# One decoder layer on one core: another order of splits, taps, scaled keys and key sums inside the loop over four heads

## The chip, the core and the metric

The kernel runs on one core of a Trainium2 chip. The metric is the device time of one execution in microseconds (us), lower is better. The core has five engines that run their own queues in order and meet through semaphores: TensorE (matrix products), VectorE and ScalarE (elementwise work), GpSimd (here mostly a queue that issues DMAs) and SyncE (the queue that loads weights).

## What is computed

One layer of a hybrid decoder on 512 prompt tokens and 8 x 4 sample tokens, model width 1024: a convolution branch and an mLSTM memory with 4 heads (value width 512, key width 256), merged by gates, then an MLP. The part that the change touches is the memory of one head:

```python
def step(carry, xs):                       # a chunk of tokens
    ...
    w_intra = jnp.exp(D - m_t[:, :, None, :])
    w_inter = jnp.exp(inter - m_t)
    s = jnp.einsum('bthk,bshk->btsh', qc, kc) * w_intra
    num = jnp.einsum('btsh,bshv->bthv', s, vc) + w_inter[..., None] * jnp.einsum('bhvk,bthk->bthv', C, qc)
    den = jnp.sum(s, axis=2) + w_inter * jnp.einsum('bhk,bthk->bth', n, qc)
    h = num / jnp.maximum(jnp.abs(den), jnp.exp(-m_t))[..., None]
    ...
    C_new = dec[..., None, None] * C + jnp.einsum('bsh,bshv,bshk->bhvk', wk, vc, kc)
    n_new = dec[..., None] * n + jnp.einsum('bsh,bshk->bhk', wk, kc)
    return (C_new, n_new, m_new), h
...
c = lax.conv_general_dilated(full, w_dw[:, None, :], ...) + b_dw     # 31 taps per channel
...
hm = hm.reshape(B, T, D_M).astype(x.dtype) * jax.nn.sigmoid(o)
```

## The kernel before

All weights come as chunks of 1024 x 128 values (512 KB) in the order of their use. SyncE loads a chunk into one of two places of `wraw`, as soon as the chunk two places ahead has been split. A **split** makes two tiles of it: ScalarE writes `whi` (line 512, a rounded copy), then VectorE writes `wlo` (line 830, what the rounding lost). Both lie in rings of four, so the split of chunk k also waits until the product of chunk k-4 is done. `split(k)` in the head loop is this pair of steps, one on each engine's queue; it runs three chunks ahead of the product. A product on TensorE is the sum of whi x ahi, whi x alo and wlo x ahi over eight slices of 128 rows.

The loop over heads has 12 chunks: q0, q1, k0, k1 (queries and keys), four for the values, and o0 to o3 (output gates), which in splits are numbers 0 to 3, 4 to 7 and 8 to 11; split(12) to split(14) are already for the next head. What each engine does in a head is written out by hand, and the engines' queues are in order. Two banks pairs of PSUM, `product0` and `product1`, are used in turn in the order of the list `USES`: a product that wants a slot waits until its last user has been drained. The order there is v3, v4, o0, cu0, cu1, o1, cu2, cu3, o2, o3, cu4, pv0, cu5, pv1, cc01, cu6, pv2, cu7, pv3, cc23, alternating between the slots.

The names around the change, in the order of TensorE's work in a head:

- **v0 to v4**: values of the four blocks of 128 prompt tokens and of the sample tokens. VectorE drains each by adding a bias into `vtok`. The sample tokens' v4 needs two adds (lines 1052 and 1054), and is copied to `vst` by ScalarE (two copies) and VectorE.
- **kw, kst**: from the transposed keys in the PSUM tile `side`, ScalarE makes `kw` (4 instructions, scaled keys of the prompt) and from the sample keys `kst` (24 instructions, each masked to the rows of one sample sequence). The **scores** (`scores()`, behind v2) overwrite the banks that kw reads, so they wait for kw.
- **pt, pts**: weights times scores, on VectorE. TensorE then sums them (den, sden).
- **taps**: the convolution of two channel blocks, 31 taps in two halves, 62 instructions of 128x512 on VectorE in each head, with nobody waiting for a single one. The tables `V_TAPS`, `O_TAPS`, `PV_TAPS` say which lie where. `sample_products` and `sample_sum` are the same convolution for the sample tokens.
- **o0 to o3**: drained by ScalarE with a sigmoid into `hm` (line 677). The first needs an activation table load.
- **cu0 to cu7**: outer products (`outer(n)`, from `vst` and `kst`) for the eight sample states; VectorE adds each to its state in `crg` (`update(n)`, line 1095), a ring of four. GpSimd stores an updated state and loads the one four places on; `readout(1)` needs states 4 to 7.
- **key sums**: 8 products of `kw` with a column of ones (two passes each, 16 matmuls).
- **pv0 to pv3**: values weighted by pt, drained by VectorE into `hr`; **cc01, cc23**: new state of the prompt.

Of the kernel before, what the change touches and what calls it, by code (L numbers as in the profile page):

```python
# [89 lines left out]
V_TAPS = [(5, 8), (8, 11), (11, 13), (13, 13)]  # L90
O_TAPS = [(16, 18), (18, 18), (18, 21), (21, 24)]
PV_TAPS = [(24, 24), (24, 26), (26, 26), (26, 28)]
# [21 lines left out]
def hybrid_layer(nc, xT, wstream, w_gates, cols, b_gates, b_v, w_dw, hist, c_in, n_in, m_in,  # L114
# [8 lines left out]
    with ctx:  # L123
# [382 lines left out]
        def _(act):  # L506
# [99 lines left out]
            with act.Fori(0, HEADS) as h:  # L606
# [3 lines left out]
                def was_drained(name):  # L610
                    wait_drained(act, h, name)

                def split(k):
                    hi(h, PERHEAD, C_HEAD + k)
# [32 lines left out]

                act.wait_ge(kh_ready, h + 1)
# [7 lines left out]
                act.wait_ge(wkp_ready, h + 1)  # L656
                for half in range(2):
                    act.wait_ge(kt_ready, 2 * h + (half + 1))
                    for q in (2 * half, 2 * half + 1):
                        act.activation(kw[:, q, :], side[:, half, DK * (q % 2):DK * (q % 2 + 1)], ACT.Copy,  # L660
                                       scale=wkp[:, q:q + 1]).then_inc(kt_used, 1)
                split(8)

                was_drained("v4")
                act.activation(vst[0:NS, :], vtok[0:NS, ST, :], ACT.Copy).then_inc(vs_hi, 1)
                act.activation(vst[64:96, :], vtok[0:NS, ST, :], ACT.Copy).then_inc(vs_all, 1)
                split(9)
# [5 lines left out]
                for k in range(VT):  # L673
                    if k == 0:
                        act.activation(warm[:, :], eps[:, :], ACT.Sigmoid).then_inc(table_in, 1)
                    s = use(f"o{k}")
                    act.activation(tile(hm, 4 * h + k), slot(s), ACT.Sigmoid, bias=c("b_o", 4 * h + k)).then_inc(drained[s], 1)
                    split(11 + k)
# [140 lines left out]
        def _(dve):  # L819
# [3 lines left out]
            def mark(ins):  # L823
                ins.then_inc(dve_step, 1)
                return st.add()
# [131 lines left out]
            with dve.Fori(0, HEADS) as h:  # L957
# [9 lines left out]
                def split(k):  # L967
                    lo(h, PERHEAD, C_HEAD + k)
# [77 lines left out]
                for s_ in range(ST + 1):  # L1046
                    s = use(f"v{s_}")
                    if s_ < ST:
                        V.tensor_tensor(vtok[:, s_, :], psum[s][:, 0, :], bv[:, :], ALU.add).then_inc(drained[s], 1)
                    else:  # L1050

                        n = mark(V.tensor_tensor(vtok[0:NS, ST, :], psum[s][0:NS, 0, :], bv[0:NS, :], ALU.add))
                        dve.wait_ge(dve_step, n)
                        V.tensor_tensor(vtok[0:NS, ST, :], psum[s][NS:2 * NS, 0, :], vtok[0:NS, ST, :], ALU.add).then_inc(drained[s], 1)
                    if s_ == 0:

                        dve.wait_ge(kh_ready, h + 1)
                        V.tensor_tensor(kwl[:, :], kws[:, :], kwh[:, :].bitcast(f32), ALU.subtract).then_inc(kl_ready, 1)
                    if s_ == 3:
                        dve.wait_ge(st_ready, 5 * h + 5)  # L1060
                        for q in range(ST + 1):
                            dve.wait_ge(w_ready, 8 * h + ST + q)
                            bank, at_ = ST_AT[q]
                            if q < ST:
                                w_ = SEQ - P * q
                                d = pt[:, PT_AT[q]:PT_AT[q] + w_]
                                V.tensor_tensor(d, d, side[:, bank, at_:at_ + w_], ALU.mult).then_inc(pt_ready, 1)  # L1067
                            else:
                                d = spread(pts[:, :])
                                V.tensor_tensor(d, d, by_quad(side[0:NS, bank, at_:at_ + NS]), ALU.mult).then_inc(pt_ready, 1)  # L1070
                    if s_ < 2:
                        taps(*V_TAPS[s_])
                    elif s_ < ST:
                        if s_ == 3:
                            dve.wait_ge(dve_step, sums_at)
                        n = sample_products(s_ - 2)
                        taps(*V_TAPS[s_])
                        sums_at = sample_sum(s_ - 2, n)
                split(8)
                dve.wait_ge(vs_hi, h + 1)  # L1080
                V.tensor_tensor(vst[NS:2 * NS, :], vtok[0:NS, ST, :], vst[0:NS, :].bitcast(f32), ALU.subtract).then_inc(ops_ready, 1)
                split(9)
                taps(13, 14)
# [5 lines left out]
                taps(14, 16)  # L1089
# [8 lines left out]
                for k in range(VT):  # L1098
                    split(11 + k)
                    if k < 2:  # L1100
                        update(2 * k)
                        update(2 * k + 1)
                    if k == 1:
                        dve.wait_ge(dve_step, sd)
                        V.reciprocal(sst[:, 1:2], sst[:, 0:1]).then_inc(srec_ready, 1)
                        dve.wait_ge(dve_step, rd)
                        rd = mark(V.reciprocal(rden[:, :], rden[:, :]))
                    taps(*O_TAPS[k])
# [16 lines left out]
                taps(28, WIDTH - 1)  # L1125
# [139 lines left out]
        def _(pe):  # L1265
# [90 lines left out]
            with pe.Fori(0, HEADS) as h:  # L1356
# [131 lines left out]
                outer(3)  # L1488
# [4 lines left out]
                ins.then_inc(np_ready, 1)  # L1493
                chunk("o2", 10)
# [158 lines left out]
```

## Time and profile before

| | us |
|---|---|
| median of 3 runs | 1370.46 |
| lowest, highest | 1367.4, 1371.08 |
| profiled execution | 1366.04 |
| its span | 1364.3 |
| TensorE busy in the span | 1279.8 (94%) |
| VectorE busy | 724.9 (53%) |
| ScalarE busy | 489.2 (36%) |

The span runs from the first to the last instruction; the execution's own time is 1.7 us longer. The four heads take 502 us of it, from 130 to 632. In the views, PE is TensorE, PEld its weight loads, DVE VectorE, ACT ScalarE, POOL GpSimd. Every matmul is put down to one helper line, 1267, so the tiles tell them apart. An idle time in brackets stands in front of the instruction that ended it, with what released it.

### The profile page before, as it was taken

To read this page: it belongs to the slowest core of one execution; us is meant where nothing else is said; L and a number is where in the kernel's file an instruction comes from. 1 tells how busy PE (TensorE), PEld (TensorE's weight loads), DVE (VectorE), ACT (ScalarE), POOL (GpSimd) and SP (SyncE) were. 2 spreads that over 40 slices of the span, in tenths; PEclk is the share of its full clock that TensorE was granted. 3 is DMA by queue.
4 is the path that set the end of the run, shared out by engine and by line. 5 is a ranking of instruction groups with operands and counts; after the bars stand their busy time and mean duration, and the time that the engine had idled before them with its cause. 6 is when DMAs were issued, how large, how long until landed. Compare 5 with 4: busy or idle time off the path is not lost.

```text
span 1364.3 us, 23810 instructions
## 1 busy us (share of the span) xinstructions
PE 1279.8 (94%) x9123; PEld 1192.2 (87%) x9123; DVE 724.9 (53%) x966; ACT 489.2 (36%) x725; POOL 81.6 (6%) x139
## 2 busy tenths in 40 slices
PE   6999998999899989989999999996999999999994
PEld 6999867887797869678999999995999999999993
DVE  4343576877687687766555533334644222444324
ACT  6333432352244236323465322234433222333121
POOL 3011101100110110011000000002000000000002
PEclk8999998999899999989999999998899999999997
DMA  6245515413450533151322222240122222223211
GB/s 184 78 127 145 96 60 173 180 60 113 148 194 15 201 146 124 59 181 69 109 78 93 80 90 78 90 160 31 62 93 92 93 84 85 86 84 93 93 46 65
DMA packets 39762, 141.19 MB, mean 103 GB/s; under 512 B 5012, under 2 KB 5524, under 8 KB 39592
## 3 DMA queue, kind: packets, MB, share of 16 engines
q1 hardware_dynamic: 27848, 99.37, 22.2%
q0 software_dynamic: 11872, 41.23, 9.1%
q8 instruction: 30, 0.49, 0.1%
q14 instruction: 12, 0.10, 0.0%
HBM read 118.31 MB, written 22.26 MB: 103 GB/s over the span
## 4 chain that ended last, share of the span: by engine, by line
PE 80%; ACT 7%; DVE 6%; issue 3%; DMA 2%; DVEq 0%; ACTq 0%; POOL 0%; POOLq 0%; SPq 0%
PE product L1267 77%; PE side L1267 4%; ACT kst L654 3%; DMA wraw<-in_wstream 2%; DVE crg L1095 1%; ACT whi L512 1%; DVE y L1211 1%; DVE wlo L830 1%; DVE accp L981 1%; ACT kw L660 0%; DVE pt L1067 0%; DVE swin L992 0%; ACT fr L520 0%; ACT L531 0%; DMA x<-in_xT 0%
## 5 line engine op out<-in xcount | busy, mean ns | idle before, releaser
L830 DVE TENSOR_TENSOR wlo<-wraw,whi 128x1024 fp32r<-128x1024 f32 x176 | 215.4, 1224 | 268.8 <-ACT whi L512 263.2
L1267 PE MATMUL product<-ahi,whi 128*128 128x256 f32 (+1 forms) x1536 | 326.5, 294 | 20.8 <-DVE alo L855 10.8
L1267 PE MATMUL product<-ahi,wlo 128*128 128x256 f32 (+1 forms) x1536 | 322.4, 291 | 0.0
L1267 PE MATMUL product<-alo,whi 128*128 128x256 f32 (+1 forms) x1536 | 321.0, 291 | 0.0
L1267 PEld LDWEIGHTS product<-ahi,whi 128*128 128x128 f32 x1536 | 251.2, 192 | 28.0 <-issue 23.5
L512 ACT ACTIVATE whi<-wraw 128x1024 fp32r<-128x1024 f32 x176 | 184.5, 1051 | 233.0 <-PE product L1267 181.5
L1267 PEld LDWEIGHTS product<-alo,whi 128*128 128x128 f32 x1536 | 251.2, 192 | 0.0
L1267 PEld LDWEIGHTS product<-ahi,wlo 128*128 128x128 f32 x1536 | 250.5, 192 | 0.0
L981 DVE SCALAR_TENSOR_TENSOR accp<-u,wdw,accp 128x512 f32<-128x512 f32 x240 | 163.4, 745 | 0.3
L1267 PE MATMUL product<-hidhi,wlo 128*128 128x256 f32 (+1 forms) x512 | 105.8, 287 | 0.0
L1267 PE MATMUL product<-hidlo,whi 128*128 128x256 f32 (+1 forms) x512 | 105.7, 288 | 0.0
L1267 PE MATMUL product<-hidhi,whi 128*128 128x256 f32 (+1 forms) x512 | 104.8, 286 | 0.0
L1267 PEld LDWEIGHTS product<-hidhi,wlo 128*128 128x128 f32 x512 | 82.0, 188 | 0.0
L1267 PEld LDWEIGHTS product<-hidhi,whi 128*128 128x128 f32 x512 | 81.9, 188 | 0.0
L1267 PEld LDWEIGHTS product<-hidlo,whi 128*128 128x128 f32 x512 | 81.2, 188 | 0.0
L793 ACT ACTIVATE fr<-fr 128x544 f32<-128x544 f32 x32 | 21.1, 659 | 113.4 <-DVE fr L1233 113.4
L1267 PE MATMUL product<-whi,ahi 128*128 128x512 f32 (+1 forms) x160 | 57.3, 358 | 2.6 <-DVE wlo L830 2.6
L1267 PE MATMUL product<-wlo,ahi 128*128 128x512 f32 (+1 forms) x160 | 56.3, 352 | 0.0
L1267 PE MATMUL product<-whi,alo 128*128 128x512 f32 (+1 forms) x160 | 56.3, 352 | 0.0
L1267 PE MATMUL product<-mhi,wlo 128*128 128x256 f32 (+1 forms) x256 | 52.9, 288 | 0.0
L1267 PE MATMUL product<-bhi,wlo 128*128 128x256 f32 (+1 forms) x256 | 52.9, 288 | 0.0
L1267 PE MATMUL product<-mhi,whi 128*128 128x256 f32 (+1 forms) x256 | 52.9, 288 | 0.0
(247 smaller groups left out, 1627.8 us busy)
## 6 DMA issues: line engine op xcount, KB each, us to landing
wraw<-in_wstream SPq DMA_DIRECT2D x176, 512.0 KB, 3.3
crg<-in_c_in POOLq DMA_DIRECT2D x32, 512.0 KB, 6.0
out_c_s<-crg POOLq DMA_DIRECT2D x32, 512.0 KB, 3.0
hb<-head_rows POOLq DMA_DIRECT2D x4, 580.0 KB, 5.4
x<-in_xT SPq DMA_DIRECT2D x4, 544.0 KB, 5.1
sgm<-in_xT SPq DMA_DIRECT2D x1, 2176.0 KB, 8.8
out_yT<-y SPq DMA_DIRECT2D x8, 272.0 KB, 2.1
out_c_p<-cst POOLq DMA_DIRECT2D x4, 512.0 KB, 7.9
```

What stands on the lines that cost most here:

```text
L512: act.activation(whi[:, k % RING, :, :], wraw[:, k % 2, :, :], ACT.Copy).then_inc(hi_done, 1)
L654: act.activation(kst[NS * q:NS * (q + 1), n, :], part, ACT.Copy, scale=own[:, b:b + 1]).then_inc(kst_ready, 1)
L793: act.activation(fr[:, 2 + k % 2, :], fr[:, k % 2, :], ACT.Square).then_inc(hidsq_ready, 1)
L830: V.tensor_tensor(wlo[:, k % RING, :, :], wraw[:, k % 2, :, :], whi[:, k % RING, :, :].bitcast(f32), ALU.subtract).then_inc(lo_done, 1)
L981: ins = V.scalar_tensor_tensor(sum_, src, w, sum_, ALU.mult, ALU.add)
L1095: V.scalar_tensor_tensor(crg[:, n % C_RING, :, :], crg[:, n % C_RING, :, :], hb[:, R_DEC + b:R_DEC + b + 1], psum[s][:, :, :], ALU.mult, A ...
L1211: V.scalar_tensor_tensor(tile(y, j), tile(y, j), c(gain, j), rst3, ALU.mult, ALU.mult).then_inc(y_scaled, 1)
L1267: return pe.matmul(out, lhsT, rhs, start=start, stop=stop, skip_group_check=check)
```

## The change

On ScalarE, kw is made ahead of kst; split(9) stands ahead of the copies of v4; in the loop over o0 to o3, split(11+k) stands ahead of the sigmoid. On VectorE, the score products pt stand behind v2 and ahead of v3's drain; split(8) stands ahead of v4's two adds and split(9) behind them; taps move by the tables and stand ahead of split(11+k) except at k = 1, where they stand between the split and the update. On TensorE the key sums move between outer(2) and outer(3). No computation is added or taken away.

```diff
-V_TAPS = [(5, 8), (8, 11), (11, 13), (13, 13)]
-O_TAPS = [(16, 18), (18, 18), (18, 21), (21, 24)]
-PV_TAPS = [(24, 24), (24, 26), (26, 26), (26, 28)]
+V_TAPS = [(5, 8), (8, 11), (11, 15)]
+O_TAPS = [(16, 17), (17, 19), (19, 23), (23, 24)]
+PV_TAPS = [(24, 24), (24, 26), (26, 26), (26, 26)]
...
                 was_drained("kts")
                 act.activation(kwh[:, :], kws[:, :], ACT.Copy).then_inc(kh_ready, 1)
+                act.wait_ge(wkp_ready, h + 1)
+                for half in range(2):
+                    ...                                            (kw, four instructions)
                 act.wait_ge(kh_ready, h + 1)
                 ...                                                (kst, 24 instructions)
-                act.wait_ge(wkp_ready, h + 1)
-                for half in range(2):
-                    ...
                 split(8)
+                split(9)
                 was_drained("v4")
                 ...
-                split(9)
...
                 for k in range(VT):
+                    split(11 + k)
                     if k == 0:
                         act.activation(warm[:, :], eps[:, :], ACT.Sigmoid).then_inc(table_in, 1)
                     s = use(f"o{k}")
                     act.activation(tile(hm, 4 * h + k), slot(s), ACT.Sigmoid, ...).then_inc(drained[s], 1)
-                    split(11 + k)
...
+                    if s_ >= 2:
+                        if s_ == 3:
+                            dve.wait_ge(dve_step, sums_at)
+                        n = sample_products(s_ - 2)
+                    if s_ < 3:
+                        taps(*V_TAPS[s_])
+                    if s_ >= 2:
+                        sums_at = sample_sum(s_ - 2, n)
-                    if s_ == 3:
+                    if s_ == 2:
                         dve.wait_ge(st_ready, 5 * h + 5)
...
                 split(8)
+                s = use("v4")
+                ...                                                (the two adds of v4)
+                split(9)
                 dve.wait_ge(vs_hi, h + 1)
                 V.tensor_tensor(vst[NS:2 * NS, :], ...).then_inc(ops_ready, 1)
-                split(9)
-                taps(13, 14)
...
-                taps(14, 16)
+                taps(15, 16)
                 split(10)
...
                 for k in range(VT):
+                    if k != 1:
+                        taps(*O_TAPS[k])
                     split(11 + k)
+                    if k == 1:
+                        taps(*O_TAPS[k])
                     if k < 2:
                         update(2 * k)
                         update(2 * k + 1)
...
-                    taps(*O_TAPS[k])
...
-                taps(28, WIDTH - 1)
+                taps(26, WIDTH - 1)
...
                 outer(2)
-                outer(3)
                 pe.wait_ge(sden_abs, h + 1)
                 ...                                                (key sums)
                 ins.then_inc(np_ready, 1)
+                outer(3)
```

In the piece of the difference for ScalarE behind the transposed sample keys, - is before and + is the change:

```order
 L646 ACTIVATE kwh<-kws 32x256
 L648 REGISTER_ALU
-L654 ACTIVATE kst<-kwh,own 32x256 x16
-L654 ACTIVATE kst<-kwl,own 32x256 x8
-L658 REGISTER_ALU
-L660 ACTIVATE kw<-side,wkp 128x256 x2
...
+L652 ACTIVATE kw<-side,wkp 128x256 x2
+L661 ACTIVATE kst<-kwh,own 32x256 x16
+L661 ACTIVATE kst<-kwl,own 32x256 x8
```

The four kw now stand in front of the 24 kst.

ScalarE before, from split(10) (the first whi) over the table load to o1 (hm of product1), with buffer numbers:

```order
L512 ACTIVATE whi_50<-wraw_49 128x1024
L675 ACT_TABLE_LOAD
L675 ACTIVATE warm_63<-eps_62 128x1
L315 REGISTER_ALU
L677 ISA
L677 ACTIVATE hm_73<-product0,col_52 128x544
L511 REGISTER_ALU
L512 ACTIVATE whi_50<-wraw_49 128x1024
L315 REGISTER_ALU
L677 ISA
L677 REGISTER_ALU
L677 ACTIVATE hm_73<-product1,col_52 128x544
```

And the same place in the change:

```order
L512 ACTIVATE whi_50<-wraw_49 128x1024
L511 REGISTER_ALU
L512 ACTIVATE whi_50<-wraw_49 128x1024
L677 ACT_TABLE_LOAD
L677 ACTIVATE warm_63<-eps_62 128x1
L315 REGISTER_ALU
L679 ISA
L679 ACTIVATE hm_73<-product0,col_52 128x544
L509 REGISTER_ALU
L512 ACTIVATE whi_50<-wraw_49 128x1024
```

Split(11), the second whi, went from behind o0's sigmoid to in front of the table load, and split(12) took its place; the later ones follow in the same way.

VectorE before, from update(2) to update(4). Between the reciprocals and the last update stand split(13), six taps, split(14) and six taps:

```order
L830 TENSOR_TENSOR wlo<-wraw,whi 128x1024
L317 REGISTER_ALU
L1095 SCALAR_TENSOR_TENSOR crg<-crg,hb,product 128x1024
...
L1105 RECIPROCAL sst<-sst 128x1
L1106 REGISTER_ALU
L1107 RECIPROCAL rden<-rden 128x512
L829 REGISTER_ALU
L830 TENSOR_TENSOR wlo<-wraw,whi 128x1024
```

And the same place in the change, where eight taps, split(13), two taps and split(14) stand between them:

```order
L982 SCALAR_TENSOR_TENSOR accp<-u,wdw,accp 128x512
L317 REGISTER_ALU
L1092 SCALAR_TENSOR_TENSOR crg<-crg,hb,product 128x1024
...
L1106 RECIPROCAL sst<-sst 128x1
L1107 REGISTER_ALU
L1108 RECIPROCAL rden<-rden 128x512
L981 REGISTER_ALU
```

Update(2) now stands behind four taps, with split(12) ahead of those and not directly in front of the update, and ten taps instead of twelve stand ahead of update(4).

## Rows read from the trace of the kernel before

**Rows 1.** The page's part 4, chain that ended last, share by engine.

```profile
PE 80%; ACT 7%; DVE 6%; issue 3%; DMA 2%; DVEq 0%; ACTq 0%; POOL 0%; POOLq 0%; SPq 0%
```

**Rows 2.** Stretches: us, busy us (instructions) by engine, TensorE clock, DMA share, GB/s.

```profile
257.90:383.00 125.10, 116.81 (x707) 97.26 (x706) 94.39 (x142) 47.04 (x85) 10.40 (x20) 0.96 0.36 128
...
341.00:344.00 3.00, 3.00 (x15) 3.00 (x14) 3.00 (x3) 0.00 (x0) 1.51 (x3) 0.50 0.90 303
```

**Rows 3.** Waits of TensorE from 256 to 381 us: total us, times, longest us.

```profile
PE product L1267 <- DVE crg L1095: 5.6, 4, 3.7
PE side L1267 <- ACT kw L660: 1.2, 1, 1.2
PE product L1267 <- DVE wlo L830: 0.6, 1, 0.6
PE product L1267 <- ACT hm L677: 0.5, 1, 0.5
```

**Rows 4.** Timeline of TensorE: start us, us, instruction, [idle us before it, releaser].

```profile
318.73 0.52 PE L1267 MATMUL product<-ahi,whi 128*128 128x256 f32 x2 [0.63 <-DVE wlo L830]
...
337.45 1.84 PE L1267 MATMUL side<-ones,kw 128*128 128x1 f32 x16
...
353.99 1.92 PE L1267 MATMUL side<-crg,qm 128*32 128x512 f32 x16
...
362.43 1.22 PE L1267 MATMUL product<-vst,kst 96*128 96x512 f32 x2 [3.70 <-DVE crg L1095]
363.45 4.47 PE L1267 MATMUL product<-pt,vtok 128*128 128x512 f32 x8
...
372.63 2.32 PE L1267 MATMUL product<-pt,vtok 128*128 128x512 f32 x8
...
375.73 2.42 PE L1267 MATMUL product<-pt,vtok 128*128 128x512 f32 x8 [0.32 <-DVE hr L1115]
```

**Rows 5.** Chain that ended last, in order of time: start us, us, what.

```profile
215.33 14.87 PE product L1267 x96
...
329.64 6.24 PE product L1267 x48
...
340.27 13.80 PE product L1267 x96
...
362.43 9.01 PE product L1267 x26
...
487.50 7.93 PE product L1267 x26
```

**Rows 6.** Timeline of ScalarE, columns as in rows 4.

```profile
289.16 6.64 ACT L654 ACTIVATE kst<-kwh,own 32x256 fp32r<-32x256 f32 x16 [0.53 <-DVE kwl L1058]
...
299.15 1.57 ACT L660 ACTIVATE kw<-side,wkp 128x256 f32<-128x256 f32 x4
...
322.04 1.06 ACT L512 ACTIVATE whi<-wraw 128x1024 fp32r<-128x1024 f32 x1 [1.62 <-DMA wraw<-in_wstream]
...
354.90 1.04 ACT L512 ACTIVATE whi<-wraw 128x1024 fp32r<-128x1024 f32 x1
```

**Rows 7.** Timeline of VectorE, columns as in rows 4.

```profile
311.48 0.69 DVE L1049 TENSOR_TENSOR vtok<-product,bv 128x512 f32<-128x512 f32 x1 [6.27 <-PE product L1267]
...
317.40 1.20 DVE L830 TENSOR_TENSOR wlo<-wraw,whi 128x1024 fp32r<-128x1024 f32 x1
...
337.80 1.22 DVE L830 TENSOR_TENSOR wlo<-wraw,whi 128x1024 fp32r<-128x1024 f32 x1 [4.46 <-ACT whi L512]
...
357.12 4.06 DVE L981 SCALAR_TENSOR_TENSOR accp<-u,wdw,accp 128x512 f32<-128x512 f32 x6
```

**Rows 8.** Timeline of GpSimd: store of the third state, load of the eighth.

```profile
340.91 0.53 POOL L451 DMA_DIRECT2D out_c_s<-crg  x1 [5.75 <-DVE crg L1095]
...
349.20 0.53 POOL L439 DMA_DIRECT2D crg<-in_c_in  x1 [3.20 <-DMA out_c_s<-crg]
```

**Rows 9.** Tile crg: us from issue of its DMAs to landing.

```profile
DMA to landing us min/median/max: 2.9/3.8/10.0
```

More of the change, by code:

```diff
@@ L646, in _ @@
                 act.activation(kwh[:, :], kws[:, :], ACT.Copy).then_inc(kh_ready, 1)
+                act.wait_ge(wkp_ready, h + 1)
+                for half in range(2):
+                    act.wait_ge(kt_ready, 2 * h + (half + 1))
+                    for q in (2 * half, 2 * half + 1):
+                        act.activation(kw[:, q, :], side[:, half, DK * (q % 2):DK * (q % 2 + 1)], ACT.Copy,
+                                       scale=wkp[:, q:q + 1]).then_inc(kt_used, 1)
                 act.wait_ge(kh_ready, h + 1)
@@ L654, in _ @@
                         act.activation(kst[NS * q:NS * (q + 1), n, :], part, ACT.Copy, scale=own[:, b:b + 1]).then_inc(kst_ready, 1)
-                act.wait_ge(wkp_ready, h + 1)
-                for half in range(2):
[L658 to L661, printed above, removed]
                 split(8)
+                split(9)
                 was_drained("v4")
@@ L1045, in _ @@
                 dve.wait_ge(bv_in, 16 * h + 16)
-                for s_ in range(ST + 1):
+                for s_ in range(ST):
                     s = use(f"v{s_}")
[L1048 to L1054, printed above, removed]
+                    V.tensor_tensor(vtok[:, s_, :], psum[s][:, 0, :], bv[:, :], ALU.add).then_inc(drained[s], 1)
                     if s_ == 0:
@@ L1070, in _ @@
                                 V.tensor_tensor(d, d, by_quad(side[0:NS, bank, at_:at_ + NS]), ALU.mult).then_inc(pt_ready, 1)
[L1071 to L1078, printed above, removed]
-                split(8)
+                split(8)
+                s = use("v4")
+                n = mark(V.tensor_tensor(vtok[0:NS, ST, :], psum[s][0:NS, 0, :], bv[0:NS, :], ALU.add))
+                dve.wait_ge(dve_step, n)
+                V.tensor_tensor(vtok[0:NS, ST, :], psum[s][NS:2 * NS, 0, :], vtok[0:NS, ST, :], ALU.add).then_inc(drained[s], 1)
+                split(9)
                 dve.wait_ge(vs_hi, h + 1)
                 V.tensor_tensor(vst[NS:2 * NS, :], vtok[0:NS, ST, :], vst[0:NS, :].bitcast(f32), ALU.subtract).then_inc(ops_ready, 1)
-                split(9)
-                taps(13, 14)
                 dve.wait_ge(den_abs, h + 1)
```

## The prediction

> **What bounds the kernel now.** The page's chain that ended last comes first: TensorE carries 80% of it, ScalarE 7%, VectorE 6% [rows 1]. So only time in which TensorE waits, or runs at its lower clock, can be won. The change lies wholly inside the loop over four heads, so I read one head, the second (257.9 to 383.0 us). TensorE is busy 116.8 us of its 125.1, at a mean clock of 0.96 [rows 2]. The list of its waits gives the rest: 5.6 us for updated states (4 waits, the longest 3.7), 1.2 for the scaled keys kw, 0.6 for a wlo, 0.5 for a sigmoid hm [rows 3]. The same waits stand in the third and fourth head to 0.1 us. Two stretches at the low clock follow from them: from 341 to 344 us it is 0.50, and the weighted values that start at 363.45 take 4.47 us where the next ones, at 372.63, take 2.32 [rows 2, 4]. The other engines have room: VectorE is busy 94.4 us, ScalarE 47.0, and the DMA share is 0.36 [rows 2]. What they lack is not time but the right order.
>
> **Edit 1, scaled keys ahead of masked ones.** On ScalarE the 24 masked keys kst run from 289.16 to 299.1, then the four kw take 1.57 us, and the scores on TensorE, which overwrite the banks kw reads, wait 1.2 us for them [rows 3, 6]. Put first, kw ends near 291 and kst near 300.8. The first outer product wants kst only at about 325, so the 1.6 us that kst loses is covered 24 us deep. **Gain 1.2.**
>
> **Edit 2, VectorE between v2 and o0.** The products of weights and scores now come ahead of v3's drain, and four more taps ahead of them. From v2's drain on VectorE has 1.2 us of window products, 8 taps at 0.68 (six take 4.06), 1.2 of sum and 1.8 of score products, 9.6 in all, from 300.4 to about 310; v3 ended at 311.4 and now ends 1.2 sooner, at 310.2 [rows 7]. So v3's drain is not late, and v4 needs only v2's bank. After v3: products and sum 2.4 us, until 313.3. TensorE ends v4 at about 313.8, and split(8) on ScalarE waits for that. VectorE's half comes at 315.0 to 316.2; before it stood behind both adds of v4 and began at 317.40 [rows 7]. TensorE's sums end at 316.9 instead of 318.1, so o0 starts at once where it waited 0.6 [rows 4]. **Gain 0.6.** The adds of v4, vst and the rounding of split(9) follow by 319.5, well ahead of the outer products.
>
> **Edit 3, rounding ahead of sigmoids.** ScalarE made chunk 11+k only after the sigmoid of o_k, although the buffers it needs are free one o chunk sooner. VectorE, which runs its queue in order, sat behind that: its half of split(11) ended at 328.2, and only then came update(0), on which o1 waits 0.6 of the 5.6 us; its half of split(12) waited 4.46 us for ScalarE and then kept update(2) back until 338.95, on which o2 waits 1.0 of them [rows 3, 7]. Now split(11) is issued before the sigmoid table is loaded. Its raw chunk is the danger: split(10) waited for a DMA until 322.04, 3.4 us after split(8) was done at 318.6 [rows 6, 7]. By the same 3.4 the raw chunk 11 is there at 318.7 + 3.4 = 322.1, ScalarE is through at 323.2, table and warm-up take it to 324.7, and o0's sigmoid ends at 325.4. The second outer product needs that at 325.6: 0.2 us to spare. VectorE has one tap (1.35) between split(10) and split(11) and ends at 325.4, the first outer product at 325.6. Update(0) ends at 326.9 and o1 starts at 327.2. **Gain 0.6**, with nothing in reserve.
>
> **Edit 4, key sums between the outer products.** Before, outer(3) waited 0.5 for o1's sigmoid [rows 3], and o2 waited for update(2) behind split(12). Now outer(2), then 1.84 us of key sums [rows 4], which hide both the sigmoid (0.7 us after o1) and update(2) (1.28 us, VectorE free since the taps ended at 332.1, o1 ending at 333.3). Outer(3) ends at about 336.3, update(2) at 335.3. **Gain 0.5 + 1.0 = 1.5**, and o2 starts near 336.3 instead of 340.27.
>
> **Edit 5, taps ahead of the late splits.** Between update(3) and update(4) VectorE has 3.4 us of reciprocals, ten taps (6.8) and two wlo (2.4). Before it had twelve taps, six of them (4.06 us from 357.12) behind split(14), whose ScalarE half came at 354.90, after o3's sigmoid [rows 6, 7]. So update(4) ended at 362.4 and the outer product behind it waited 3.7 us [rows 4]. Now both ScalarE halves are done before VectorE asks (o1 ended at 333, o2 at 342.4), and the queue is empty at 337.6 + 12.8 = 350.4. The fifth outer product is ready at 350.9 (o3 ends at 348.4, read-out 1.9, outer 0.6 [rows 4]), so TensorE is now the later one. Update(4) ends at 352.2, the weighted values at 353.1. **Gain 3.7.** What is late next is hr for the second weighted product: VectorE needs 0.7 us after the first ends, as the third and fourth show with 0.32 [rows 4]. **Loss 0.2.** Everything behind keeps its distances, VectorE's last ten taps too.
>
> **The clock.** Two low stretches go with the waits. o2 and o3 together take 13.80 us from 340.27, where o1 alone takes 6.24: 1.3 too much; in the first head 14.87, 2.4 too much [rows 5]. The later one costs 4.47 - 2.32 = 2.15, and some 0.5 of the outer product's 1.22: 2.6 [rows 4]. In the third head that piece is 7.93 instead of 9.01, so 1.5; the first is like it [rows 5]. Bounds: nothing is won if the clock falls as before, all of it if it holds. The stretch with little work on TensorE around the key sums shrinks from 335.7-340.3 (4.6 us, 1.5 of them waits) to 3.0 without a wait. The nearest row is the stretch from o0's end to o1 (324.9 to 329.6, 4.7 us with a 0.6 wait, all of it narrow or short work), after which o1 takes its 6.24 at full clock [rows 5]. I take the whole gain. The Trainium skill (TensorE: Matmul & The Clock Gate, HAM oscillation) says that gaps between bursts make the gate fall and the next burst starts cold; the 4.47 us behind the wait of 3.7 agree. By that rule alone, which counts gaps, both stretches would go too.
>
> **The sum.** Second and fourth head: 1.2 + 0.6 + 0.6 + 1.5 + 3.7 - 0.2 = 7.4, with clock 1.3 + 2.6 = 11.3 each. Third: 7.4 + 1.3 + 1.5 = 10.2. First: 7.4 + 2.4 + 1.5 = 11.3. Together 44.1 us. From the profiled execution's 1366.04 us that leaves 1321.9. The median of the runs is 1370.46, 4.4 higher; so I expect 1326 as the median.
>
> **Rivals.**
> 1. *The clock still falls after the key sums.* For it: they are sixteen one-column matmuls, now directly before the last outer product and o2. Against: no wait is left there. It gives back 3 x 1.3 + 2.4 = 6.3: 1332.5.
> 2. *Split(11) is late.* For it: 0.2 us of reserve, and ScalarE now holds o0's sigmoid and a table load behind a DMA; every 0.1 us over is lost at o1. If the raw chunk takes 1.5 us more than the 3.4, four heads lose 5 us: 1331. Against: the read-out, and not a queue, sets the first outer product, and state transfers start only after update(0).
> 3. *The state transfers become the bound (slower).* Read-out of the second four states needs the eighth state's load, which follows two updates, a save and a load on GpSimd's queue. Before, save 2 was issued at 340.91 and load 7 at 349.20 [rows 8], and TensorE read at 353.99. Now save 2 goes out at 336.0, so load 7 at about 344.3, landing 3 to 4 us later, and the read-out comes at 348.4: some 0.5 us left where about 1.5 stood. Landings range from 2.9 to 10.0 us, median 3.8 [rows 9]. If save 3 and load 7 each took 10, load 7 would land at 338.5 + 10 + 10 = 358.5 and TensorE would wait 10.1 us; with the 2.6 of low clock behind such a wait that is 12.7 a head against 11.3 won: 1376. It is slower from about 9 us of wait on. Against: the raw chunk 14 now travels at 330 instead of among these (the queue was full there), so they should be faster, not slower. The Trainium skill (DMA: Bandwidth & Descriptors, Issuing engines are not separate DMA queues) says that transfers of all issuers interleave on the same 16 engines, which is why moving that chunk helps. A mild form, 2 us late with the clock falling, loses 4.6 a head at most: 1344.
> 4. *The reordering doesn't reach the big wait.* Should VectorE lose over 0.5 us between update(3) and update(4), that is a loss one for one; a full 1.5 us gives 1332, a cold clock with it 1338.
>
> **How the numbers follow.** Forecast (1326, own range 1322 to 1330) 0.58; rival 1 0.14; rival 2 0.10; rival 4 0.06; mild rival 3 (1344) 0.06; hard rival 3 (1376) 0.03; others below 1322 0.03. The range takes in the forecast and rivals 1, 2 and half of 4: 1320 to 1336. A measurement tells about 0.3% (4 us) from no change. Faster 0.95, same 0.02, slower 0.03.
>
> **What would show it.** In the second head: no wait for kw before the scores; o0 right behind the sums; o2 at about 336; no wait of over 1 us for an updated state; the clock at 1.00 from 336 to 372; the head at 114 us instead of 125.1; split(11) waiting for a DMA in place of split(12) waiting for a sigmoid. Wrong would be a wait of the read-out for a load, a low clock behind the key sums, or new waits before o1.

## The result, and the profile after

The changed kernel takes 1316.18 us in the median of four runs (1315.46 to 1318.25), against 1368.93 for the kernel before in the same comparison (1362.68 to 1371.08). The ratio is 0.9624, 95% interval 0.9589 to 0.9659. A second comparison gave 1320.60 against 1369.22, ratio 0.9645 (0.9628 to 0.9661). I had forecast 1326, within 1320 to 1336: the sign and the places of the gain were right, the gain was forecast too small, and 1316.18 lies below the range. The changed kernel's own times differ between the two comparisons by 4.4 us; its runs do not overlap (1315.46 to 1318.25, and 1318.90 to 1321.31).

The span of the profiled execution went from 1364.3 to 1315.1 us, 49.2 where the sum said 44.1. The page's busy times and its chain of work that ended last, answering to [rows 1]:

```profile
PE 1259.8 (96%) x9123; PEld 1177.6 (90%) x9123; DVE 724.8 (55%) x966; ACT 489.0 (37%) x725; POOL 81.6 (6%) x139
...
PE 91%; DVE 3%; ACT 2%; DMA 2%; issue 1%; POOL 0%; POOLq 0%; ACTq 0%; DVEq 0%; SPq 0%
```

TensorE's share of the chain rose from 80 to 91%. It does the same 9123 matmuls in 20.0 us less busy time, nearly all of it low clock that is gone: the mean granted clock rose from 0.969 to 0.983. The other 29.2 of the 49.2 us are idle time. The stretches of the second to fourth head, from one q0 to the next (columns as in [rows 2]):

```profile
242.56:355.37 112.81, 111.87 (x706) 93.89 (x706) 94.26 (x142) 46.93 (x85) 10.39 (x20) 1.00 0.41 141
355.37:468.22 112.85, 111.92 (x707) 93.91 (x706) 94.35 (x142) 46.91 (x85) 10.39 (x20) 1.00 0.41 143
468.22:581.16 112.94, 111.93 (x707) 93.92 (x706) 94.36 (x142) 46.91 (x85) 7.84 (x15) 1.00 0.40 139
```

Each head is near 112.9 us where it was 125.1, with the clock at 1.00. VectorE's 94.3 and ScalarE's 46.9 us of work are the same. All that TensorE still waits for in the second head, answering to [rows 3]:

```profile
PE product L1267 <- DVE hr L1115: 0.7, 2, 0.3
PE product L1267 <- DVE crg L1092: 0.3, 1, 0.3
```

The waits for kw, wlo, hm and three of the four for crg are gone; the first wait for hr is new (0.33, as forecast), the second and the remaining crg stood there before. TensorE's timeline, answering to [rows 4]:

```profile
317.63 0.62 PE L1267 MATMUL product<-vst,kst 96*128 96x512 f32 x2
318.09 1.84 PE L1267 MATMUL side<-ones,kw 128*128 128x1 f32 x16
319.80 0.71 PE L1267 MATMUL product<-vst,kst 96*128 96x512 f32 x2
...
332.41 1.92 PE L1267 MATMUL side<-crg,qm 128*32 128x512 f32 x16
...
336.91 0.70 PE L1267 MATMUL product<-vst,kst 96*128 96x512 f32 x2
...
337.94 2.42 PE L1267 MATMUL product<-pt,vtok 128*128 128x512 f32 x8 [0.33 <-DVE hr L1115]
```

The outer product that waited 3.70 us now starts straight behind the first weighted product. ScalarE and VectorE at the same place, answering to [rows 6, 7]:

```profile
304.04 1.06 ACT L512 ACTIVATE whi<-wraw 128x1024 fp32r<-128x1024 f32 x1 [0.20 <-DMA wraw<-in_wstream]
306.58 1.06 ACT L512 ACTIVATE whi<-wraw 128x1024 fp32r<-128x1024 f32 x1 [1.48 <-DMA wraw<-in_wstream]
307.65 1.28 ACT L677 ACT_TABLE_LOAD   x1
```

```profile
318.29 1.28 DVE L1092 SCALAR_TENSOR_TENSOR crg<-crg,hb,product 128x1024 f32<-128x1024 f32 x1 [2.22 <-PE product L1267]
...
335.04 1.28 DVE L1092 SCALAR_TENSOR_TENSOR crg<-crg,hb,product 128x1024 f32<-128x1024 f32 x1 [1.09 <-PE product L1267]
```

Split(11) waits for its DMA, as foreseen, and updates 2 and 4 now wait for TensorE, not TensorE for them. GpSimd, answering to [rows 8, 9], has its eighth load out at 328.02, and no wait followed. Against the prediction the transfers did not get faster: the median landing went up from 3.8 to 4.6 us, and this eighth load took 3.6 us in both kernels:

```profile
320.26 0.53 POOL L451 DMA_DIRECT2D out_c_s<-crg  x1 [4.28 <-DVE crg L1092]
...
328.02 0.54 POOL L439 DMA_DIRECT2D crg<-in_c_in  x1 [3.22 <-DMA out_c_s<-crg]
```

And from the view of the state tile, the time of its GpSimd transfers from issue to landing:

```profile
DMA to landing us min/median/max: 2.9/4.6/10.0
```

### The profile page after: what moved, and what is told of

The parts are those of the page before. It is cut to its first block, busy times and chain, and to the rows that moved or that the text cites. A ratio compares the mean times of both kernels' runs of the same rounds, so it can differ in the third digit from the quotient of the medians.

```text
span 1315.1 us, 23810 instructions
## 1 busy us (share of the span) xinstructions
PE 1259.8 (96%) x9123; PEld 1177.6 (90%) x9123; DVE 724.8 (55%) x966; ACT 489.0 (37%) x725; POOL 81.6 (6%) x139
## 4 chain that ended last, share of the span: by engine, by line
PE 91%; DVE 3%; ACT 2%; DMA 2%; issue 1%; POOL 0%; POOLq 0%; ACTq 0%; DVEq 0%; SPq 0%
PE product L1267 85%; PE side L1267 6%; DMA wraw<-in_wstream 1%; DVE y L1211 1%; DVE hr L1115 0%; DVE crg L1092 0%; ACT whi L512 0%; DMA x<-in_xT 0%; ACT fr L520 0%; ACT L531 0%; DVE wlo L831 0%; PE side L1416 0%; ACT rst L529 0%; ACT L527 0%; ACT sqh L707 0%
## 5 line engine op out<-in xcount | busy, mean ns | idle before, releaser
L1267 PE MATMUL product<-ahi,whi 128*128 128x256 f32 (+1 forms) x1536 | 323.0, 292 | 11.3 <-DVE alo L856 10.8
L1267 PE MATMUL product<-alo,whi 128*128 128x256 f32 (+1 forms) x1536 | 317.5, 288 | 0.0
L1267 PEld LDWEIGHTS product<-ahi,whi 128*128 128x128 f32 x1536 | 248.2, 190 | 18.1 <-issue 17.5
L1267 PEld LDWEIGHTS product<-alo,whi 128*128 128x128 f32 x1536 | 247.9, 190 | 0.0
L1267 PEld LDWEIGHTS product<-ahi,wlo 128*128 128x128 f32 x1536 | 247.0, 189 | 0.0
```

Source lines behind the costliest of these rows:

```text
L1267: return pe.matmul(out, lhsT, rhs, start=start, stop=stop, skip_group_check=check)
```

## The experiments

All comparisons of parts go by the second head's period, from the start of its key transposes on TensorE to the next head's, since this leaves out what happens before the heads. It is 125.06 us in the kernel before, 112.82 in the changed one; "the changed kernel" is its first profiled execution where nothing else is said. The variants from edit 1 undone to the key sums twice were executed once each, so their whole times carry the difference between executions, and their periods say more. Of "o2 and o3" I give the time from o2's start to the start of the second read-out: at full clock it is 12.07 us.

**Both kernels once more.** No edit.

> The kernel before, unchanged, in a second profiled execution. It asks how much of the 49.2 us between the two spans (1364.3 and 1315.1) is the change and how much is where TensorE's clock happened to fall. Theory A (the change alone): the span is 1364 again to 0.5 us, and the low stretches of the first head (4.6 us at 155.7, 7.8 us for o1 at 203) come back as they were. Theory B (part of the low clock comes and goes with the execution): the waits come back to 0.1 us, but the low stretches behind them are of other lengths; I expect the span within 1358 to 1367 and at least one of the three (first head's v0, first head's o1, start of the memory gate at 690) to be different.

> The changed kernel, unchanged, in a second profiled execution and timed. Both theories: the head period of heads two to four is 112.8 to 113.0 us again, since no low clock is left in them. Theory B: the slow start of the gate products at 640 us (1.5 us longer than before) is absent or elsewhere. Time 1314 to 1318 us; ratio to the kernel before 0.962. The kernel before in the same job tells whether the 4.4 us that I put between a profiled execution and the median stands: if it doesn't, its profiled and timed runs differ by under 2 us.

The kernel before took 1370.43 us with a span of 1368.7, 4.4 more than the first time. Its three later heads:

```profile
258.97:384.05 125.08, 116.77 (x706) 97.20 (x706) 94.38 (x142) 47.03 (x85) 10.41 (x20) 0.96 0.37 128
384.05:510.11 126.06, 118.37 (x706) 98.74 (x706) 94.27 (x142) 47.05 (x85) 10.38 (x20) 0.95 0.37 127
510.11:636.23 126.12, 118.23 (x706) 98.53 (x705) 94.28 (x142) 47.04 (x85) 7.82 (x15) 0.95 0.36 125
```

The first execution had 125.06, 124.00 and 125.1 there. So 3.1 of the 4.4 us lie in the third and fourth head; almost all of it is busy time at lower clock (o2 and o3 took 14.44 and 14.54 us where they took 13.71 and 13.73). Of the rest, 1.1 stood already where the second head begins, and 0.2 came behind the heads. The waits came back to 0.1 us, but for o2's, 0.37 and 0.57 in place of 0.98 in those two heads. Theory B holds, for the length of the low stretches; a span of 1368.7 is beyond what I gave it. I had also named three places, and there little moved: v0 of the first head took 4.31 us instead of 4.62, o1 of the first head 7.79 instead of 7.78, and the gate's start was as before (239.58 and 239.59 us in the chain's longest piece). So the low clock at the first head's o1 came back and is no accident of one execution.

The changed kernel took 1320.60 us, outside my 1314 to 1318, with a span of 1318.3. Its second and third head have 113.06 and 113.00 us, where outer(1) waits 0.17 to 0.23 for o0's sigmoid, and most of the 3.2 us is in the first head: a weight wait of 3.74 instead of 2.92 ahead of v0, slow values behind it, and 0.7 us more up to the second head. The gate's slow start was there again (241.12), against theory B.

**Edit 1 undone.** kw behind kst.

```diff
-                (kw, four instructions)
                 for q in range(3):
                     ...                       (kst, 24 instructions)
+                (kw, four instructions)
```

> The changed kernel with edit 1 alone undone: kw behind kst on ScalarE. Theory I (a wait is worth the idle time that the profile shows): each head longer by 1.2 us, 4.8 in all. Theory R (a wait is worth its idle time and some 0.25 us in which TensorE fills up again): 1.45 a head, 5.8 in all, with 1.2 us shown as the wait. Neither expects a low clock.

```profile
290.70 1.52 PE L1267 MATMUL side<-qT,kT 128*128 128x512 f32 x3 [1.24 <-ACT kw L660]
```

The wait is shown as 1.24 us. From the transposes (277.03) to the scores it is 13.67 us against 12.23 in the changed kernel, so 1.44 more, and the scores themselves take 0.08 more (4.73 against 4.65 to the next value block). The period is 114.49, 1.4 more than the 113.06 of the changed kernel's second execution and 1.7 more than the 112.82 of its first; the whole execution took 1326.92 us. Its clock has no low stretch in this head. This is theory R in its size: a wait costs more than the idle time that is shown. Most of the difference is how the idle time is counted: from the modelled end of the last matmul, and that end overlaps the next start when nothing waits. In the changed kernel the last value product ahead of the scores ends at 284.20 and the scores already start at 284.04, so 0.16 us of the 0.2 to 0.3 are this overlap. That TensorE has to fill up again, as theory R says, is not shown for the rest.

**Edit 4 undone.** Outer(3) ahead of the key sums.

```diff
                 outer(2)
+                outer(3)
                 ...                           (key sums)
-                outer(3)
```

> The changed kernel with edit 4 alone undone: outer(3) again ahead of the key sums. Outer(3) then waits for o1's sigmoid (0.54 us shown, 0.8 by theory R), while update(2) is done in either case under the key sums, so o2 doesn't wait for it. Forecast of the prediction: plus 0.5 a head and the clock holds. Rival: the clock falls at o2 again, since the key sums are then the last thing ahead of it with a wait before them; then 1.3 to 2.4 more a head, 1.8 to 3.2 in all a head. A state wait at o2 instead would show update(3), not update(2), as late.

```profile
323.55 0.74 PE L1267 MATMUL product<-vst,kst 96*128 96x512 f32 x2 [0.55 <-ACT hm L679]
```

```profile
326.00:332.00 6.00, 6.00 (x37) 6.00 (x37) 6.00 (x6) 0.00 (x0) 1.25 (x3) 0.72 0.93 293
212.00:218.00 6.00, 6.00 (x50) 6.00 (x50) 6.00 (x6) 0.00 (x0) 1.45 (x3) 1.00 0.88 271
```

The first fence is the timeline of TensorE, the second holds stretches at o2 in the second and in the first head. The sigmoid wait is back, and o2 starts 3.45 us behind outer(2) instead of 2.71: 0.74 more for the 0.55 shown. The clock fell in the second and fourth head (o2 and o3 13.69 and 13.69 us) and held in the first and third (12.16, 12.15), in one and the same execution. The second and third head have periods of 115.34 and 113.88, and the execution took 1325.26 us. Forecast and rival were both half right.

**ScalarE's part of edit 3 undone.** Sigmoid first, then split(11+k).

```diff
                 for k in range(VT):
-                    split(11 + k)
                     ...                       (table load at k = 0, sigmoid of o_k)
+                    split(11 + k)
```

> The changed kernel with the ScalarE part of edit 3 alone undone: sigmoid of o_k first, then split(11+k). VectorE's split(12) stands ahead of four taps and update(2), so update(2) waits for the split that follows o1's sigmoid: ready at about 318.6 + 1.1 + 1.2 + 2.7 (taps) on the head's scale where it is ready at 318.3 now, so o2 starts 5 us late. Forecast: each head longer by 5 to 7 us, 20 to 28 in all, with waits for states at o2 of 3 to 5 us and a low clock behind. Rival (the taps, not the order on ScalarE, carry the gain): under 2 us a head.

```profile
333.83 0.82 PE L1267 MATMUL product<-ahi,whi 128*128 128x256 f32 x2 [4.34 <-DVE crg L1092]
```

o2 waits 4.34 us for update(2), and o2 and o3 then take 13.77 us: the period is 119.42, 6.6 us a head more, as forecast. The execution took 1345.37 us.

**VectorE's taps over o0 to o3 back.** Splits and updates first, then taps, with the old table.

```diff
-O_TAPS = [(16, 17), (17, 19), (19, 23), (23, 24)]
+O_TAPS = [(16, 18), (18, 18), (18, 21), (21, 24)]
...
                 for k in range(VT):
-                    if k != 1:
-                        taps(*O_TAPS[k])
                     split(11 + k)
-                    if k == 1:
-                        taps(*O_TAPS[k])
                     ...                       (updates, reciprocals)
+                    taps(*O_TAPS[k])
```

> The changed kernel with VectorE's order over o0 to o3 as before (split, updates, then the taps 16-18, none, 18-21, 21-24), ScalarE's order kept. Forecast: splits are early anyway, so VectorE only has one tap pair moved; update(4) comes after 3.4 of reciprocals, 12 taps (8.1) and 2.4 of splits, 13.9 us behind update(3), at about 335.7 in the second head where cu4 is ready at 334.9: a wait of about 1 us more at outer(5), 1 us a head, and up to 0.5 won at o1. Rival (the tap tables carry the gain): 4 us a head or more comes back.

```profile
333.45 1.92 PE L1264 MATMUL side<-crg,qm 128*32 128x512 f32 x16 [0.51 <-DMA crg<-in_c_in]
```

The period is 113.38, 0.56 more, and not by the way I gave: no wait for update(4) appeared, but the read-out waited 0.51 us for the load of the eighth state. Split(13) now stands straight behind the reciprocals, so the weight chunk that its place waits for is loaded among the state transfers: SyncE issues it 54.5 us behind the head's transposes, where the changed kernel does at 59.8. The eighth load itself goes out at the same place of the head (56.2 us behind the transposes in both, at 328.53 here and at 328.02 in the changed kernel), but takes 4.8 us to land instead of 3.6. This is rival 3 in small: what the taps ahead of the split do here is to hold a DMA back. The wait is there in three of the four heads (0.2, 0.5 and 0.5 us). The execution took 1318.07 us, which can't be told from the changed kernel. So VectorE's order over o0 to o3 carries little of the gain: with twelve taps back ahead of update(4) its wait of 3.7 us did not return.

**Edit 2 undone on VectorE.** Score products behind v3, split(8) behind v4's adds, split(9) behind vst, taps 13 to 16 after it.

```diff
-V_TAPS = [(5, 8), (8, 11), (11, 15)]
+V_TAPS = [(5, 8), (8, 11), (11, 13), (13, 13)]
...
-                for s_ in range(ST):
+                for s_ in range(ST + 1):
                     ...                       (v4's adds inside, score products at s_ = 3)
                 split(8)
-                ...                           (v4's adds)
-                split(9)
                 ...                           (vst)
+                split(9)
+                taps(13, 14)
                 ...                           (rden, sst)
-                taps(15, 16)
+                taps(14, 16)
```

> The changed kernel with edit 2 alone undone on VectorE: score products behind v3, split(8) behind both adds of v4, split(9) behind vst, taps 13-16 there. ScalarE keeps split(9) early. Forecast: o0 waits 0.6 us again for split(8) (theory I 0.6, theory R 0.85), and everything behind it up to update(0) is later by 2.7 us of taps, so o1 waits some 1 us more for update(0): 1.5 to 2.5 us a head, 6 to 10 in all.

```profile
PE product L1271 <- DVE crg L1096: 1.2, 2, 1.0
PE product L1271 <- DVE hr L1119: 0.6, 2, 0.3
PE product L1271 <- DVE wlo L831: 0.6, 1, 0.6
```

```profile
314.80:322.30 7.50, 7.50 (x48) 7.50 (x49) 4.83 (x6) 0.45 (x1) 1.63 (x3) 0.78 0.92 330
```

The waits are as forecast, 0.64 for split(8) and 0.96 more at o1, and behind the second the clock fell: o1 took 7.57 us where it took 6.11. Period 116.16, 3.3 more, which is above my 1.5 to 2.5 by that low stretch (second fence, mean clock 0.78). The execution took 1326.42 us.

**Edit 3 alone, on ScalarE alone.** The kernel before with split(11+k) ahead of the sigmoid, nothing else.

```diff
                 for k in range(VT):
+                    split(11 + k)
                     ...                       (table load at k = 0, sigmoid of o_k)
-                    split(11 + k)
```

> The kernel before with one thing changed: on ScalarE split(11+k) stands ahead of the sigmoid of o_k. If ScalarE's order carries the gain at o2 and at update(4), this alone gives 5 to 9 us a head: split(12) is ready when VectorE asks, update(2) no longer waits for it, and split(13), split(14) don't hold update(4) back. The wait of 3.7 us at outer(5) should shrink to 1.5 or less with 12 taps and two splits behind update(3). In all 1328 to 1345 us. Rival (the parts need each other): under 3 us a head, above 1350.

```profile
PE product L1267 <- ACT hm L678: 1.3, 2, 0.8
PE side L1267 <- ACT kw L660: 1.3, 1, 1.3
PE product L1267 <- DVE hr L1115: 0.7, 2, 0.3
PE product L1267 <- DVE wlo L830: 0.6, 1, 0.6
PE product L1267 <- DVE crg L1095: 0.3, 1, 0.3
```

1341.65 us, period 119.82: this one move gives 5.2 of the 12.2 us of this head, and 24.4 of the 49.2 us between the profiled spans (1364.3 to 1339.9). It takes away the wait of 3.7 us wholly and both waits for updates at o1 and o2; the taps had not moved. So the gain that the prediction put down to edit 5, taps ahead of the late splits, comes with ScalarE's order alone. But the clock still falls, and in three heads harder than before: o2 and o3 take 14.93 us in this head, 14.81 and 14.69 in the later two, behind key sums with waits for two sigmoids ahead of them. In the first head it held, and there the read-out waited 1.2 us for a state load, rival 3 again in small.

**Key sums twice.** The changed kernel with the same 16 one-column matmuls repeated in place.

```diff
-                for kk in range(QT):
+                for kk in (0, 1, 0, 1):
```

> The changed kernel with the key sums computed twice at the same place (16 one-column matmuls more, the same result). It asks whether the clock can fall with TensorE busy but doing narrow work. Theory C (only waits let the clock fall): o2 and o3 keep their 12.07 us, each head grows by the second set alone, 1.7 us (16 at 106 ns), 6.8 in all. Theory D (narrow work counts as little work, and the shorter stretch around the key sums is what keeps the clock up): the low clock is back at o2 in most heads, 1.5 to 2.8 more each, 13 to 18 us in all.

```profile
324.84 0.62 PE L1267 MATMUL product<-vst,kst 96*128 96x512 f32 x2
325.30 3.63 PE L1267 MATMUL side<-ones,kw 128*128 128x1 f32 x32
328.79 1.18 PE L1267 MATMUL product<-vst,kst 96*128 96x512 f32 x2
329.77 0.66 PE L1267 MATMUL product<-ahi,whi 128*128 128x256 f32 x2
```

TensorE does not wait anywhere in these rows, and still the outer product behind the sums takes 1.18 us instead of 0.71. The granted clock is the third number from the end in these stretches:

```profile
325.30:328.80 3.50, 3.50 (x34) 3.50 (x32) 1.28 (x1) 1.61 (x2) 1.06 (x2) 1.00 0.30 123
328.80:332.20 3.40, 3.40 (x15) 3.21 (x15) 2.19 (x3) 0.00 (x0) 0.22 (x1) 0.50 0.83 278
```

It was 1.00 over the key sums and 0.50 right behind them: the clock fell while TensorE was busy with narrow work. o2 and o3 took 13.40, 13.18, 13.04 and 14.51 us in the four heads. The period is 116.30, 3.5 more, where the work itself is 1.8 (3.63 less 1.84); the execution took 1333.77 us. Theory D: the clock is not lost to waits alone. In three of the four heads the loss at o2 and o3 is smaller than the 1.5 us that I had given it.

**Two attempts to go further.** e10 loads the sigmoid table ahead of split(11); e11 adds to this that one half of the key sums goes between outer(5) and the second weighted product.

```diff
                 for k in range(VT):
-                    split(11 + k)
                     if k == 0:
                         act.activation(warm[:, :], eps[:, :], ACT.Sigmoid).then_inc(table_in, 1)
+                    split(11 + k)
```

> The changed kernel with the sigmoid table load and its warm-up ahead of split(11) on ScalarE, so that they no longer stand behind its DMA. The outer(1) that waited 0.2 to 0.3 us for o0's sigmoid should not wait: 0.3 to 0.5 us a head by theory R, 1 to 2 in all. If the wait stays, it was split(11) itself, 1.1 us of ScalarE in front of the sigmoid, that is late.

> As e10, and only half of the key sums between outer(2) and outer(3); the other half fills the wait for hr between outer(5) and the second weighted product. Expected: 0.85 us less ahead of o2 as long as update(2) is done (it ends 1.94 us after outer(2) begins, the half stretch is 1.9 long: no slack), and 0.9 added at the second place against 0.33 of wait and 0.25 of filling up that it hides: 0.3 to 0.5 us a head better than e10, 1 to 2 in all, the clock at full.

```profile
PE product L1267 <- DVE hr L1115: 0.3, 1, 0.3
PE product L1267 <- DVE crg L1092: 0.3, 1, 0.3
PE side L1267 <- DMA crg<-in_c_in: 0.2, 1, 0.2
```

The fence is e11's waits of its second head. e10 has a period of 112.57, 0.25 less than the changed kernel, and no wait for the sigmoid; e11 has 112.50. The half sums moved save 0.71 ahead of o2 (2.00 us from outer(2) instead of 2.71), cost 0.33 at the second place, and o2 and o3 take 12.42, with the read-out now waiting 0.17 for a state load. Timed, e10 has 1316.97 us (ratio 0.9623, 0.9598 to 0.9648) and e11 1317.75 (0.9619, 0.9595 to 0.9643): neither can be told from the changed kernel. For e11 I had expected 0.3 to 0.5 us a head beyond e10, and its second head is 0.07 shorter.

## Why the prediction was right in kind and wrong in size

The second head, step by step, from starts on TensorE in the two timelines. Forecast and measured, in us:

| stretch | before | after | gain | forecast |
|---|---|---|---|---|
| transposes to first sums (edit 1) | 27.73 | 26.20 | 1.53 | 1.2 |
| first sums to read-out (edit 2) | 9.98 | 9.18 | 0.80 | 0.6 |
| read-out to o1 (edit 3) | 4.72 | 4.33 | 0.39 | 0.6 |
| o1 to o2 (edit 4) | 10.63 | 8.82 | 1.81 | 1.5 |
| o2 to second read-out (clock) | 13.72 | 12.07 | 1.65 | 1.3 |
| read-out to outer(5) (edit 5) | 8.44 | 4.50 | 3.94 | 3.7 |
| outer(5) to next transposes (clock, new wait) | 49.84 | 47.72 | 2.12 | 2.4 |
| head | 125.06 | 112.82 | 12.24 | 11.3 |

The forecast of 1326 was 1366.04 - 44.1 + 4.4, and 1316.18 was measured, 10.1 less. 5.0 of these are the last term, the way from the profiled execution to the median (below); 5.1 are the sum.

**In every head: a wait was priced at its idle time.** The four rows of edits 1, 2, 4 and 5 are 0.2 to 0.3 us above their forecast for this reason, and the clock row as well, where I had taken twice o1's 6.24 us, which holds two overlapped ends. The undone edit 1 shows it by itself (1.24 shown, 1.5 paid). With the two rows that came out lower it is 0.9 us a head, 2.8 in the later three. The names of the edits in the table are the prediction's: the experiments put the 3.94 of edit 5 down to ScalarE's order of edit 3, since it comes with that alone and doesn't leave when the taps go back.

**In the sum, most: the first head, taken to be like the second.** It gained 15.8 us, by the start of its value block after the weight wait (155.74 before, 156.16 after) to the next head's q0, against 11.3. The 0.9 of every head is in this too; two low stretches and a longer wait were not in the sum. The chain before and then after:

```profile
155.74 4.62 PE product L1267 x24
...
203.16 7.78 PE product L1267 x48
```

```profile
156.16 3.02 PE product L1267 x24
```

The values behind the weight wait ran slowly before (4.62 us) and fast after (3.02). The change doesn't touch that place, and in the repeat of the changed kernel it was slow too (4.19 us from 156.91 to the transposes, where the first execution had 2.86), as it was in nine of all thirteen profiled executions: 1.6 us of luck. o1 at 203.16 took 7.78 where other heads have 6.24, 1.5 us of low clock behind a wait of 1.15 instead of 0.63, and these do belong to the change: the repeat of the kernel before has them again (7.79), neither execution of the changed kernel has them (6.1); the rows for them were in the view that I had read for its later entries.

**Luck, perhaps, on the other side.** Behind the heads the changed kernel lost 1.8 us, 1.5 of it where the gate products start, where the granted clock is 0.50 from 639.7 to 643.1:

```profile
639.86 241.11 PE product L1267 x1920
```

It is 239.59 in the kernel before. Of thirteen profiled executions the two of the kernel before have 239.6, and of the eleven others five have 241.1, two 240.1 to 240.2 and four 239.6. So it may be more than luck, but kernels with nearly the same order of a head are on both sides, and the runs don't settle it. The parts add up: 44.1 + 2.8 (later heads) + 4.5 (first head) - 0.4 (its later start) - 1.8 = 49.2.

**The step that failed most: from the profiled execution to the median.** I added 4.4 us, the distance of the profiled execution from the median, as if it were outside the heads. The repeated profile of the kernel before, 4.4 us longer, shows what such a distance is made of: 3.1 of it were longer low stretches in the heads, which the change takes away in the typical execution as well: the changed kernel's profiled 1316.78 us lies 0.6 above its median and not 4.4 below. (The second comparison gives the change 48.6 us between medians, the first 52.8, so this is shown for the place of the 4.4 us and not to the microsecond.) Without that addition the forecast would have been 1322, with the first head's low stretch and longer wait read out as well (1.5 and 0.5) 1320.

**What was right.** All five places, the signs of all, o2's start relative to its head, the new wait of 0.33 for hr, and that VectorE's last update would be ready as TensorE's product is. Rival 1 was not met in the changed kernel, but its mechanism is real: undoing edit 4 brings the low clock back in two heads of four, and doubling the key sums in all four. The reserve of 0.2 us in rival 2 was used up: raw chunk 11 let ScalarE start at 306.58, and the outer products took 0.3 us more (1.50 for the two, read-out to o1 gains 0.39 instead of 0.6). One other row came out below its forecast, the last. There the low clock gave the 2.6 us that I had put (0.5 at the outer product, 2.1 at the weighted values and the new state behind it), but the new wait for hr, put at 0.2, cost 0.5: from outer(5) to the second weighted product it is 1.03 us, where it is 0.55 in front of the third, which doesn't wait. This is the same mistake of price, on the side of the losses. Rival 3 didn't come in the changed kernel, and appeared with 0.51 us when the taps went back; what I had held against it, that the state transfers would be faster, was wrong (median landing 4.6 us instead of 3.8).

**What stays open.** Why the clock falls in one head and holds in the next with the same instructions (edit 4 undone) was not settled; the runs show only that the state of the clock at such places is not fixed by the order alone. The same holds for the slow start of the gate products.

## What to carry to other kernels

When TensorE is the bound and the other engines have spare time, read for each of its waits what stood ahead of the releaser in that engine's queue; moving the splits ahead of the sigmoids on ScalarE gave 5.2 us of 125 here with no work removed. Price a wait at what the same two products are apart where nothing waits; here that is its idle time and 0.2 to 0.3 us more. Look behind each wait, and behind each stretch of narrow products, for a low clock that goes with it; a distance between a profiled execution and the median may be made of the same low stretches. Read every pass of a loop, the first above all, before multiplying one.

## What the runs showed of the hardware

The clock fell without any wait, in a stretch of TensorE's work with one-column products (3.63 us of them at a granted clock of 1.00, then 0.50, and 1.18 us instead of 0.71 for an outer product). The Trainium skill (TensorE: Matmul & The Clock Gate, What's actually happening) says that a monitor sets the clock by how busy TensorE has recently been; the fall behind the waits goes with that, but this one came in rows that show TensorE as busy throughout, so being busy in the profile's sense was not enough here. The same instructions at the same place came out at either level in heads of one execution (o2 and o3 12.16, 13.69, 12.15 and 13.69 us with edit 4 undone). And two executions of the kernel before differed by 4.4 us in their spans with waits that were nearly the same.
